# Second block of a two-block transformer kernel: the input projection is cut into other column groups, its last two units run inside attention, and the compression follows the fourth unit

## The reference

```
proj = h @ w_in                                   # 1024 x 2844
(fq, fk, fv, ff, nq, kc, vc, ks, vs, kw, vw, ng, dq, dk, dv) = jnp.split(proj, splits, axis=-1)
log_f = jax.nn.log_sigmoid(ff + b_forget)
o_fox = fox_attention(heads(fq, 4), heads(fk, 4), heads(fv, 4), log_f)
gates = jax.nn.sigmoid(ng + b_nsa_gate).reshape(B, S, NSA_HEADS, 3)
o_nsa = nsa_attention(rope(nq, 8), rope(kc, 2), heads(vc, 2), rope(ks, 2), heads(vs, 2),
                      rope(kw, 2), heads(vw, 2), gates, cmp_pos_k, cmp_w1_k, ...)
o_dil = dilated_attention(rope(dq, 4), rope(dk, 4), heads(dv, 4))
mix = jnp.concatenate([o_fox, o_nsa, o_dil], axis=-1) @ w_out
```

## Time and profile before

| what | value |
|---|---|
| median of 3 runs | 1745.23 us (1739.86 to 1746.18) |
| the profiled execution | 1744.03 us, span 1742.3 us |
| mean granted TensorE clock | 0.984 of full |
| busy, TensorE / weight load / VectorE / ScalarE / GpSimd | 96% / 79% / 67% / 49% / 8% |
| chain that ended last | TensorE 72%, VectorE 15%, ScalarE 5%, DMA 3% |
| HBM read | 321 MB, 185 GB/s over the span |

### The profile page before, as it was taken

How to read it: one execution, slowest core, us unless ns; L and a number is a source line. 1 busy time by engine, 2 the same in 40 slices (tenths; PEclk the granted TensorE clock), 3 DMA queues, 4 the chain that set the end, 5 groups by cost and what they waited for, 6 DMA issues and landing times.

```text
span 1742.3 us, 24788 instructions
## 1 busy us (share of the span) xinstructions
PE 1675.5 (96%) x9283; PEld 1370.3 (79%) x9283; DVE 1171.3 (67%) x2012; ACT 854.5 (49%) x1500; POOL 143.3 (8%) x297
## 2 busy tenths in 40 slices
PE   7999999999999999999999999989999999899998
PEld 3897775689878786764799878757998787579986
DVE  5776555866766975547745676666788766567885
ACT  3454453455443442651555354575555544755542
POOL 0210101000000000210000010041000100410000
PEclk8999999999999999999999999899999998999999
DMA  9887335557845975336465646605655466046552
GB/s 343 302 280 265 117 97 166 188 200 246 299 157 199 340 246 169 121 98 227 145 213 190 193 148 219 179 1 163 198 185 182 159 217 182 1 144 206 183 184 83
DMA packets 185912, 323.71 MB, mean 186 GB/s; under 512 B 13540, under 2 KB 101184, under 8 KB 185792
## 3 DMA queue, kind: packets, MB, share of 16 engines
q1 hardware_dynamic: 183200, 320.54, 55.9%
q10 hardware_dynamic: 2592, 1.57, 0.3%
HBM read 321.02 MB, written 1.05 MB: 185 GB/s over the span
## 4 chain that ended last, share of the span: by engine, by line
PE 72%; DVE 15%; ACT 5%; issue 3%; DMA 3%; POOL 2%; SPq 0%; DVEq 0%; POOLq 0%; ACTq 0%
PE bank L746 68%; DVE ring_r L1832 6%; PE bank L755 3%; ACT sm L1464 2%; POOL sm L672 1%; DMA ring<-in_w_in 1%; DVE ada L1944 1%; ACT high L1378 1%; DVE gates_r L1857 1%; DVE sm L2024 1%; DMA ring<-in_w_ada 1%; DMA ring<-in_w_ff 1%; ACT sm L1396 0%; DVE oT L1908 0%; DVE wide L1825 0%
## 5 line engine op out<-in xcount | busy, mean ns | idle before, releaser
L1832 DVE TENSOR_TENSOR ring_r<-ring,high 128x1024 fp32r<-128x1024 f32 (+3 forms) x390 | 460.6, 1197 | 267.7 <-ACT high L1378 259.7
L1378 ACT ACTIVATE high<-ring 128x1024 fp32r<-128x1024 f32 (+3 forms) x390 | 402.0, 1037 | 480.9 <-PE bank L746 352.8
L746 PE MATMUL bank<-ring_r,featT_r 128*128 128x512 f32 (+3 forms) x928 | 355.3, 383 | 0.0
L746 PE MATMUL bank<-high,featT_r 128*128 128x512 f32 (+3 forms) x712 | 276.2, 388 | 9.1 <-DVE ring_r L1832 3.0
L746 PE MATMUL bank<-featT_r,high 128*128 128x256 f32 x960 | 272.9, 284 | 0.0
L746 PE MATMUL bank<-featT_r,ring_r 128*128 128x256 f32 x960 | 271.6, 283 | 0.0
L746 PE MATMUL bank<-oT_r,high 128*128 128x256 f32 x960 | 271.6, 283 | 0.0
L746 PE MATMUL bank<-high,oT_r 128*128 128x512 f32 (+3 forms) x712 | 270.0, 379 | 0.0
L746 PE MATMUL bank<-high,gates_r 128*128 128x512 f32 x736 | 230.2, 391 | 3.6 <-DVE ring_r L1832 2.6
L746 PEld LDWEIGHTS bank<-ring_r,featT_r 128*128 128x128 f32 x928 | 175.8, 189 | 26.9 <-issue 0.5
L746 PEld LDWEIGHTS bank<-oT_r,high 128*128 128x128 f32 x960 | 184.2, 192 | 0.6 <-issue 0.5
(11 more groups left out here) (270 smaller groups left out, 2156.0 us busy)
## 6 DMA issues: line engine op xcount, KB each, us to landing
ring<-in_w_ff SPq DMA_DIRECT2D x128, 512.0 KB, 4.6
ring<-in_w_ada SPq DMA_DIRECT2D x96, 512.0 KB, 5.8
ring<-in_w_up SPq DMA_DIRECT2D x176, 256.0 KB, 3.4
ring<-in_w_in SPq DMA_DIRECT2D x64, 464.0 KB, 5.3
ring<-in_w_in SPq DMA_DIRECT2D x48, 512.0 KB, 5.1
ring<-in_w_in SPq DMA_DIRECT2D x48, 474.0 KB, 5.0
ring<-in_w_down SPq DMA_DIRECT2D x44, 512.0 KB, 3.4
ring<-in_w_out SPq DMA_DIRECT2D x24, 512.0 KB, 4.9
```

Of the source, the lines that this page charges most:

```text
L746: ins = pe.matmul(o, a, b, start=start, stop=stop, skip_group_check=True)
L1378: act.activation(it["high"], it["raw"], ACT.Copy).then_inc(high_ready, 1)
L1832: dve.tensor_tensor(it["low"], it["raw"], it["high"].bitcast(F32), ALU.subtract).then_inc(low_ready, 1)
```

## The change

The columns of w_in are grouped anew: units of 512, 512, 512, 512, 398 and 398 columns, the second and the fourth from two ranges each. The compression's inputs (kc, vc) are now in unit 1, the forget gate in unit 2. The compression's weights come behind unit 3 in the stream, units 4 and 5 behind them. TensorE runs units 0 to 3, then compression, then all turns but the dilated ones, then four quarters of unit 4, and the other twelve quarters inside attention, two each in steps 0, 1, 2, 3, 5 and 6. Jobs are now in the order fox, NSA, dilated; dilated queries and keys are rotated in step 7 and turned in step 8. The compressed branch is added with the window branch instead of the selected one. ScalarE and VectorE follow with their instructions; unit 5's high parts go to spare places.

```diff
-IN2_W = N_IN // 6
+IN2_COLS = [[(FQ, FV)], [(FV, FG), (KC, KS)], [(FG, FG + 512)], [(FG + 512, KC), (KS, KS + 508)],
+            [(KS + 508, KS + 906)], [(KS + 906, N_IN)]]
+IN2_W = [sum(c1 - c0 for c0, c1 in cols) for cols in IN2_COLS]
...
+        spare_5 = [big_r[:, 0, n:n + 2 * IN2_W[5]] for n in range(T * N_IN, T * N_IN + 6 * IN2_W[5], 2 * IN2_W[5])] + [high_5[:, :]]
...
-            for u in range(6):
-                split(w_in_2[l], (IN2_W * u, IN2_W * u + IN2_W), spare=spare_2 if u == 0 else None)
+            for u in range(4):
+                split(w_in_2[l], *IN2_COLS[u], spare=spare_2 if u == 0 else None)
             plain(*[cols_piece(w[l], k0, k0 + 4, (0, CMP_H)) for k0 in range(0, 16, 4) for w in (cw1_k, cw1_v)])
+            for u in range(4, 6):
+                split(w_in_2[l], *IN2_COLS[u], spare=spare_5 if u == 5 else None)
...
+        IN_2_FILL, IN_2_READ = {0: 2, 1: 2, 2: 2, 3: 2, 5: 2, 6: 2}, (2, 4, 7)
+        DIL_ROPE, DIL_TURNS = 7, 8
+        OUT_HIGH, OUT_LOW = {7: 0, 8: 1, 9: 3, 10: 5, 12: 7}, {8: 0, 9: 1, 10: 3, 11: 5, 13: 7}
...
-                for u in range(2, 6):
-                    tokens_by_quarters((for_act, for_dve), blocks_turned if u == 4 else None, 3)
-                    if u == 4:
-                        seen.more(fox_lf)
...
-                seen.more(ready_dve)
-                turns(nsa_turns + fox_turns, wait=False)
+                def gate_sums():
+
+                    seen.more(fox_lf)
...
+                tokens_by_quarters((for_act, for_dve), blocks_turned, 3)
+                tokens_by_quarters((for_act, for_dve), gate_sums, 3)
+                quarters = gate_quarters(2)
                 seen.more(win_ready)
...
+                def first_fill():
+
+                    some_quarters(quarters, 4)
+                    hidden_back()
+
                 seen.more(ready_dve)
-                turns(key_turns + dil_turns, hidden_back)
+                turns(fox_turns + nsa_turns + key_turns, first_fill)
+                dil_turned = []
+
+                def filled(i):
+
+                    some_quarters(quarters, IN_2_FILL.get(i, 0))
+                    if i == DIL_TURNS:
+                        seen.more(ready_dve)
+                        turns(dil_turns, wait=False)
+                        dil_turned.extend((r, made[id(r)]) for r in (for_act, for_dve))
...
-                for u in range(1, 6):
-                    if u < 5:
-                        highs(4)
+                for u in range(1, 4):
+                    highs(4)
                     if u == 1:
                         continue
...
                 act.wait_ge(for_act.read, got[0])
                 act.sem_inc(evac_act, 1)
...
                 seen.more(evac_act)
+                grouped_queries(1)
+                for base in (KS, KW):
+                    v = proj2[:, :, base:base + GRP * HD].rearrange("p t (h e) -> p t h e", e=HD)
+                    rope(v[:, :, :, 0:8], v[:, :, :, 8:16], 24, 8, (0, T, GRP))
                 dve.sem_inc(ready_dve, 1)
+                turns_out(fox_turns + nsa_turns + key_turns)
...
+                    elif i == DIL_ROPE:
+                        stored(outputs)
+                        v = proj2[:, :, DQ:DQ + 2 * DIL * HD].rearrange("p t (h e) -> p t h e", e=HD)
+                        rope(v[:, :, :, 0:8], v[:, :, :, 8:16], 24, 8, (0, T, 2 * DIL),
+                             ada[:, :, :].rearrange("p a (b n) -> p (a b) n", b=2))
+                        dve.sem_inc(ready_dve, 1)
+                    elif i == DIL_TURNS + 1:
+                        turns_out(dil_turns)
```

272 lines of the change are left out of this document (148 added, 124 removed).

## The result

The changed kernel takes 1772.28 us (median of 4 runs, 1766.78 to 1776.75), the kernel before 1743.78 (median of 4). The ratio is 1.0164, 95% interval 1.0144 to 1.0185: slower by some 28 us, outside the range of the prediction. The profiled execution took 1776.75 us, the slowest of the four, with a span of 1775.0 and a mean clock of 0.974.

The account below looks back on a forecast made before the run. TensorE's column work was taken as the bound nearly everywhere, except in the second block's attention. 1744.03 - 8.6 for both layers + 7.0 for the clock gave 1742.4 us profiled, 1744 as median; range 1727 to 1759.

Parts of the forecast that it names:

- straight part, work: From the projection's second token tile to attention, TensorE work alone takes 48.4 us a layer, against 65.0 before.
- first wait: TensorE idles 2.8 us ahead of the cumulative gate sums, until VectorE finishes log-forget; ends 0 to 4.
- second wait: TensorE idles 4.5 us between compression and turns, behind unit 4's loads, roundings and lows, then VectorE's rotations; ends 2 to 6.
- steps 0 to 6, full clock: Early attention with fills: TensorE bounds, 31.3 us of work plus 1.0 for hand-overs, 32.3 against 31.01 before.
- steps 7 to end, full clock: Late attention, held by a chain: 28.0 us against 24.16, from dilated rotation, weight passes and a low.
- lower clock: One clock fall a layer, behind the second wait across turns and first fill, 3.5 us; none for the first wait.
- Widths: Regrouping w_in's columns: six units of 48 matmuls go from 62.4 to 61.0 us, worth only 1.4.
- Rival (c): Long clock fall behind the second wait, over turns, fill and fox steps: 1754, or 1758 with a short first-wait fall; chance 0.19.
- the forecast's 1.3: In steps 0 to 6, 13.0 us of fill cost 1.3 us if the clock stays at 2.4 GHz.
- The weight passes' part: The dilated jobs, now last, put their four weight passes, 1.2 us, each in the last chain.
- The lows next to GpSimd's scaling: One low of the output projection stands in the last attention chain, counted at 1.2 us on VectorE.
- Rival (d): In filled attention steps, fills sharing output-ring banks wait for VectorE's copies: +5.5 us a layer, 1755; chance 0.12.

Follow-up runs that it names:

- e5: Changed kernel with log-forget gate early on VectorE and unit 3's store ahead of pieces 2 and 3 of unit 4; ratio to the kernel before 1.0019.
- e3: Changed kernel with 512-column matmuls, results never read, added on TensorE ahead of its waits in the second block; ratio to the kernel before 1.0069.
- e1: Changed kernel with the forget gate's sum and log-forget moved earlier on VectorE, ahead of compression windows and query rotation; ratio to the kernel before 1.0124.
- e2: Changed kernel with unit 3's store ahead of pieces 2 and 3 of unit 4 on ScalarE and VectorE; ratio to the kernel before 1.0087.
- e4: Changed kernel with the output projection's first two roundings and lows moved from the last steps to steps 6, 7 and 9; ratio to the kernel before 1.0148.
- e8: Changed kernel with all sixteen quarters of units 4 and 5 ahead of attention instead of four; ratio to the kernel before 1.0198.
- e6: e5 with e4's edit and never-read 512-column matmuls added ahead of waits inside attention alone; ratio to the kernel before 0.9938.
- e9: e5 with e4's edit, no added matmuls; ratio to the kernel before 1.0018.
- e14: e9 with the dilated rotation ahead of an output copy in step 7, and seven VectorE instructions of the compressed softmax left out; ratio to the kernel before 0.9951.
- e15: e9 with the dilated rotation ahead of an output copy in step 7, and the dilated jobs' weight passes left out; ratio to the kernel before 0.9947.
- e13: Kernel before with four idle stretches of TensorE put ahead of later quarters of units 2 and 4, 1.42 to 3.86 us; ratio to the kernel before 1.0076.
- e16: Kernel before with four idle stretches of TensorE, two inside unit 2 and two ahead of the gate sums; one execution, 1763.55 us beside 1740.04.
- e17: e16 with the gap lengths of the two layers exchanged; one execution, 1765.93 us beside 1740.04.
- e11: e9 with the dilated rotation ahead of an output copy in step 7, and never-read matmuls added inside attention; ratio to the kernel before 0.9950.
- e7: Kernel before with 16 never-read 512-column matmuls added ahead of waits in steps 1, 2 and 5; ratio to the kernel before 0.9998.

## Why the prediction was wrong, step by step

The two new waits were forecast by name and stand where the forecast had them. What failed is the clock term first of all, then the price of the filled steps, then the length of the second wait. First layer, us:

| term | forecast | measured | where |
|---|---|---|---|
| straight part, work | 48.4 | 49.3 | e5 |
| first wait | 2.8 | 2.69 | changed |
| second wait | 4.5 | 6.26 (6.63 in the second layer) | changed |
| steps 0 to 6, full clock | 32.3 | 36.8 | e3 |
| steps 7 to end, full clock | 28.0 | 30.3 | e3 |
| lower clock | 3.5 | 11.4 (10.4) | changed less e3 |

The measured column adds up to 136.8, 1.2 more than the 135.6 measured: its terms come from three runs, and e3's straight part (57.1) is 1.1 shorter than e5's with both waits added.

- **Widths and straight work: right.** 49.3 for 48.4.
- **First new wait: right** in place and size (e1 takes it away by the order alone).
- **Second new wait: right in mechanism** (e2), 1.8 to 2.1 us too small. The range 2 to 6 didn't hold it: the load took 5.19 us and not 3.8, and that is 1.4 of the 1.8. (In e1, e4 and e8, with the same order, it was 5.4 to 7.3 us, by turns inside and outside that range.)
- **Clock: the step that failed most**, 3.5 us forecast and 11.4 and 10.4 measured. "None for the first wait" is wrong: in both layers of the changed kernel that wait was followed by 6 us at 0.50, and in 7 of 8 layers of all runs that had it. "3.5 a layer behind the second wait only" left out attention, where four gaps of 1.3 to 3.6 us each brought a fall; e6 against e9 puts three or four such falls at 7 us a layer. In the earlier trace rows a gap of 1.98 us had 3.8 us at the lower clock behind it. Read as the price of every gap of that size, it would have put a fall behind both new waits and asked what gaps attention would have. Rival (c) came nearest in time (1754 to 1758) but had one long stretch behind the second wait; what happened was six short ones. The Trainium skill, "TensorE: Matmul & The Clock Gate", Part 1, says activity lifts the throttle again; the trace agrees in that each fall in the changed kernel was over within 7.5 us of its gap's end. The short kind came true, and their number, six a layer, made it dear.
- **Steps 0 to 6: 32.3 forecast, 36.8 at full clock.** By e8 the fills cost 10.6. That isn't to be held against the forecast's 1.3, which is what 13.0 us of fill cost less what the clock gives back; by the forecast's own figures at full clock, 32.3 with them and 23.5 (the chain) without, they cost 8.8. The forecast took TensorE as the only bound there and gave 1.0 for hand-overs. At full clock 36.8 us stand against 34.9 busy in e3, 1.8 of which are added matmuls: 3.8 us are waits, and e14 names their source, VectorE's row in steps 2 to 4 (the compressed softmax beside two copies of quarters and an output). In the earlier trace rows VectorE is busy 18.28 of 31.01 there, and that average hid it. The rest of the excess is work: 33.1 us of it instead of 31.3. And without a full clock, which the forecast took for granted here, the changed kernel needed 39.4.
- **Steps 7 to the end:** 28.0 forecast, 30.3 at full clock. The weight passes' part was seen and is real (1.8 us, e15). The lows next to GpSimd's scaling were counted at 1.2; e4 puts their worth at 0 to 1.4. What holds the rest of the 6 us over the kernel before (30.3 for 24.2), and what the new order of jobs alone costs, no run parts.
- **Rival (d)** had filled steps bind worse through banks: the place was right, and the size (some 7 us a layer at full clock for its 5.5); the reason, banks, was right only in part.

The chances gave 0.25 to slower. Nearly all errors went one way, and the terms were added as if independent, while each of the six waits of a layer also brought a fall.

One reading of the rows was loose: the 17.4 us at the lower clock "in each layer" are one stretch in the first layer; in the second they are one of 13.8 and one of 3.4 us. The sum is the same, so no term moves by it.

## What to carry to other kernels

Price a gap of TensorE of 2 us or more at itself plus some 2 us (an estimate: 1.7 to 2.7 for each fall, from e3, e13, e16 and e17), and a shorter one, down to 1.2, at itself and perhaps that: of those of 1.22 to 1.38 us counted above 16 of 26 brought a fall, of those of 1.46 to 1.84 us none of 18. Then count the gaps: a change that turns one bound stretch into several short waits loses more than the waits. Before moving work into the idle time of a chained stretch, read what the chain's slowest engine does in each step and not its mean busy share, since an engine at 60% on average can be full in the very steps that are to be filled. A wait can be covered by matmuls whose results nobody reads: here that alone was worth 14 to 16 us of 1750 where three to six falls a layer went with it (e6, e3), 5 us where two did (e11), and nothing in the kernel before (e7). With the two orders mended as well the change beat the kernel before by 0.6%.
